# Summing the last 24 upward tiles of a PEER layer from two halves of 512-column matmuls

## What is computed

```python
def blk(args):
    xb, ib, gb = args
    a = jnp.einsum('tkd,td->tk', u_tab[ib], xb, preferred_element_type=f32)
    a = jax.nn.gelu(a, approximate=False) * gb
    return jnp.einsum('tk,tkd->td', a.astype(xb.dtype), v_tab[ib])
```

## Time and profile before

| | |
|---|---|
| median of 3 runs | 1940.96 us (1940.9 to 1941.74) |
| the profiled execution | 1938.03 us |
| its span, from the first to the last instruction | 1936.0 us, mean granted clock 0.994 |
| TensorE busy (matmul) | 1899.6 us, 98% of the span |
| VectorE busy | 1459.9 us, 75% |
| ScalarE busy | 1123.1 us, 58% |
| DMA | 480.75 MB, mean 248 GB/s |

### The profile page before, as it was taken

One profiled execution on the slowest core, in us unless ns is written; L12 is line 12 of the kernel. 1 busy time (PEld: TensorE's weight loads), 2 busy tenths in 40 slices (PEclk: granted clock), 3 DMA queues, 4 the chain that ended last, 5 costly groups with the idle time before them and its releaser, 6 DMA issues.

```text
span 1936.0 us, 41169 instructions
## 1 busy us (share of the span) xinstructions
PE 1899.6 (98%) x11552; PEld 1678.1 (87%) x11552; DVE 1459.9 (75%) x3771; ACT 1123.1 (58%) x2217; POOL 456.1 (24%) x321
## 2 busy tenths in 40 slices
PE   7998999999999999999999999999999999999998
PEld 6848988899999888888888798889999998888887
DVE  5666699987774788888875658899777467777776
ACT  2035468876555555555555555887655555555554
POOL 1000000777776000000000000056777720000000
PEclk9999999999999999999999999999999999999998
DMA  9956388997779999999983235789877988888884
GB/s 381 375 217 251 110 283 283 276 240 196 175 174 222 334 365 360 363 358 360 316 295 89 110 131 180 226 232 237 203 176 174 215 270 268 262 266 268 261 267 166
DMA packets 251005, 480.75 MB, mean 248 GB/s; under 512 B 57120, under 2 KB 156704, under 8 KB 246960
## 3 DMA queue, kind: packets, MB, share of 16 engines
q1 hardware_dynamic: 205536, 426.21, 66.3%
q0 software_dynamic: 45392, 53.60, 12.2%
HBM read 426.10 MB, written 53.61 MB: 248 GB/s over the span
## 4 chain that ended last, share of the span: by engine, by line
PE 95%; ACT 2%; DVE 1%; issue 1%; DMA 0%; SPq 0%; ACTq 0%; DVEq 0%
PE bank L595 94%; ACT big L1115 1%; PE bank L731 0%; DMA raw<-in_x 0%; DVE raw L1337 0%; DVE big L1345 0%; ACT big L1133 0%; DVE wmod_ring L1345 0%; ACT hi L1064 0%; DVE big L1439 0%; ACT L1208 0%; DVE raw L1345 0%; ACT raw L1053 0%; ACT L1184 0%; ACT hi L1184 0%
## 5 line engine op out<-in xcount | busy, mean ns | idle before, releaser
L1639 DVE TENSOR_TENSOR lo<-raw,hi 128x512 fp32r<-128x512 f32 x1024 | 705.6, 689 | 307.1 <-ACT hi L1184 294.3
L595 PE MATMUL bank<-x_both,hi 128*128 128x256 f32 (+1 forms) x3984 | 880.8, 310 | 5.1 <-issue 2.2
L1184 ACT ACTIVATE hi<-raw 128x512 fp32r<-128x512 f32 x1024 | 645.1, 631 | 384.2 <-PE bank L595 375.2
L595 PEld LDWEIGHTS bank<-x_both,hi 128*128 128x128 f32 x3984 | 648.0, 191 | 47.4 <-issue 2.8
L595 PE MATMUL bank<-x_both,lo 128*128 128x256 f32 x2440 | 685.7, 281 | 0.0
L534 POOL DMA_INDIRECT g_store<-far_gate,far_at x256 | 423.5, 1654 | 394.7 <-DVE far_at L1631 246.2
L595 PEld LDWEIGHTS bank<-x_both,lo 128*128 128x128 f32 x2440 | 463.8, 190 | 0.0
L595 PE MATMUL bank<-hi,a_hi 128*128 128x512 f32 x1024 | 398.4, 389 | 0.0
L595 PE MATMUL bank<-lo,a_hi 128*128 128x512 f32 x1024 | 398.4, 389 | 0.0
L595 PE MATMUL bank<-hi,a_lo 128*128 128x512 f32 x1024 | 398.4, 389 | 0.0
L595 PEld LDWEIGHTS bank<-hi,a_hi 128*128 128x128 f32 x1024 | 192.2, 188 | 40.0
(11 more groups left out here) (170 smaller groups left out, 1404.2 us busy)
## 6 DMA issues: line engine op xcount, KB each, us to landing
raw<-in_u SPq DMA_DIRECT2D x256, 512.0 KB
raw<-in_v SPq DMA_DIRECT2D x256, 512.0 KB
s_store<-work SPq DMA_DIRECT2D x256, 128.0 KB
wmod_ring<-s_store SPq DMA_DIRECT2D x256, 128.0 KB, 3.6
wmod_ring<-in_w_mod SPq DMA_DIRECT2D x54, 512.0 KB, 5.1
big<-in_w_mod SPq DMA_DIRECT2D x40, 512.0 KB, 6.4
big<-in_w_q POOLq DMA_DIRECT2D x16, 1024.0 KB, 5.5
g_store<-zero SPq DMA_DIRECT2D x2, 8192.0 KB, 30.7
```

Of the source, the lines that this page charges most:

```text
L595: return nc.tensor.matmul(o, w, x, start=start, stop=stop, skip_group_check=free)
L1184: f(hi[:, r % 2, c], raw[:, r, c], ACT.Copy).then_inc(s[l]["hi_done"], 1)
L1639: v.tensor_tensor(lo[:, r % 2, c], raw[:, r, c], hi[:, r % 2, c].bitcast(F32), ALU.subtract).then_inc(s[l]["lo_done"], 1)
```

## The change

The 24 tiles of the tail take the wide form. `WIDE_ALL` is now the number of wide tiles in a layer, 56 + 24 = 80, and semaphores that count wide tiles go by it; `skipped` takes out the 48 narrow tiles between. The core of the diff:

```diff
+TAIL_AT = GROUP_AT + GROUPS
+WIDE_ALL = WIDE_TILES + NKEY - TAIL_AT
...
                     for r in range(4):
                         up(GROUP_AT + 4 * i + r, r % 2)
                         group(4 * i + r, r)
-                with pe.Fori((GROUP_AT + GROUPS) // 2, NKEY // 2) as i:
-                    for r in range(2):
-                        up(2 * i + r, r)
                 pe.wait_ge(s[l]["g_copied"], GROUPS)
+                for r in range(4):
+                    wide(TAIL_AT + r, r, False)
+                with pe.Fori(TAIL_AT // 4 + 1, NKEY // 4) as i:
+                    for r in range(4):
+                        wide(4 * i + r, r, True, TAIL_AT - WIDE_TILES)
+                pe.wait_ge(s[l]["s_sum"], WIDE_ALL * (l + 1))
                 down(0, 0, first=True)
...
-                up_steps(GROUP_AT + GROUPS, NKEY - 4)
                 for r in range(4):
-                    up_step(NKEY - 4 + r, r, NKEY // 4 - 1)
+                    wide_step(TAIL_AT + r, r, TAIL_AT // 4, True, r >= 1, TAIL_AT - WIDE_TILES)
+                with act.Fori(TAIL_AT // 4 + 1, NKEY // 4 - 1) as i:
+                    for r in range(4):
+                        wide_step(4 * i + r, r, i, True, True, TAIL_AT - WIDE_TILES)
+                for r in range(4):
+                    wide_step(NKEY - 4 + r, r, NKEY // 4 - 1, True, True, TAIL_AT - WIDE_TILES)
+                    if r == 3:
+                        sum_gelu(NKEY - 1, 3, TAIL_AT - WIDE_TILES)
                     if r >= 2:
                         split_a(r - 2, r, r - 2, False)
...
+                for r in range(4):
+                    for half in range(2):
+                        lower(TAIL_AT + r, r, half)
+                    if r >= 2:
+                        sum_halves(TAIL_AT + r - 2, r - 2, TAIL_AT - WIDE_TILES)
+                with dve.Fori(TAIL_AT // 4 + 1, NKEY // 4) as i:
                     for r in range(4):
                         for half in range(2):
                             lower(4 * i + r, r, half)
+                        sum_halves(4 * i + r - 2, (r + 2) % 4, TAIL_AT - WIDE_TILES)
                 dve.wait_ge(s[l]["g_copied"], GROUPS)
                 gates_in(0, 0)
                 for n in range(2):
                     weigh(n, n, 0)
+                    sum_halves(NKEY - 2 + n, n + 2, TAIL_AT - WIDE_TILES)
```

More of the change, by code:

```diff
@@ L867, in experts, with wide @@
             def experts(l):
-                def wide(n, r, wait=True):
+                def wide(n, r, wait=True, skipped=0):
                     if wait:
-                        pe.wait_ge(s[l]["s_sum"], n - 3 + WIDE_TILES * l)
+                        pe.wait_ge(s[l]["s_sum"], n - skipped - 3 + WIDE_ALL * l)
                     o = bank[r][:, :]
@@ L937, in experts @@
                     up(GROUP_AT - 2 + r, r)
-                pe.wait_ge(s[l]["s_sum"], WIDE_TILES * (l + 1))
+                pe.wait_ge(s[l]["s_sum"], WIDE_TILES + WIDE_ALL * l)
                 for r in range(4):
@@ L1190, in half_sum, with sum_gelu, wide_step @@
                     f(work[:, r, :], bank[r][:, T:2 * T], ACT.Copy).then_inc(s[l]["s_half"], 1)
-                def sum_gelu(n, r):
-                    act.wait_ge(s[l]["s_sum"], n + 1 + WIDE_TILES * l)
+                def sum_gelu(n, r, skipped=0):
+                    act.wait_ge(s[l]["s_sum"], n - skipped + 1 + WIDE_ALL * l)
                     f(work[:, r, :], work[:, r, :], ACT.Gelu).then_inc(s[l]["s_gelu"], 1)
-                def wide_step(n, r, round_, wait=True, before=True):
+                def wide_step(n, r, round_, wait=True, before=True, skipped=0):
                     nr, nround = (r + 2) % 4, round_ + (r + 2) // 4
@@ L1201, in wide_step @@
                     if before:
-                        sum_gelu(n - 1, (r + 3) % 4)
+                        sum_gelu(n - 1, (r + 3) % 4, skipped)
                 def gelu(n, r, round_, wait=True):
@@ L1712, in experts, with sum_halves @@
                             lower(tile, tile, half)
-                def sum_halves(n):
-                    dve.wait_ge(s[l]["s_half"], n + 1 + WIDE_TILES * l)
-                    v.tensor_tensor(work[:, n % 4, :], bank[n % 4][:, 0:T], work[:, n % 4, :], ALU.add).then_inc(s[l]["s_sum"], 1)
+                def sum_halves(n, r, skipped=0):
+                    dve.wait_ge(s[l]["s_half"], n - skipped + 1 + WIDE_ALL * l)
+                    v.tensor_tensor(work[:, r, :], bank[r][:, 0:T], work[:, r, :], ALU.add).then_inc(s[l]["s_sum"], 1)
                 for n in range(GROUP_AT - 2):
                     if 1 <= n <= WIDE_TILES:
-                        sum_halves(n - 1)
+                        sum_halves(n - 1, (n - 1) % 4)
                     for half in range(2):
@@ L1739, in experts @@
                         one_hot(4 * i + r, r)
-                with dve.Fori((GROUP_AT + GROUPS) // 4, NKEY // 4) as i:
+                for r in range(4):
[4 more added lines that the diff above has]
+                with dve.Fori(TAIL_AT // 4 + 1, NKEY // 4) as i:
                     for r in range(4):
```

## The result

The changed kernel took **1951.85 us** in the median of 6 runs (1948.66 to 1953.75), the kernel before 1940.93 us (1939.05 to 1942.45) beside it: a ratio of 1.0055, with a 95% interval of 1.0042 to 1.0068. That is 8 to 13 us slower. The forecast was slower by 7.3 us, with 1951.0 as the upper end of the range; the direction was right, the time lies 0.85 us above the range. The profiled run took 1951.48 us, with a span of 1949.7; of before 1938.03 and 1936.0.

A forecast was written before the change was run, and what follows sets the result against it. TensorE was taken to bound the kernel, unbroken from the gate groups through the downward pass. Pace -5.1, start +2.0 and ends +7.9 gave +4.8, with the clock +7.3: 1948.2 us against the median of 1940.96, range 1943.0 to 1951.0.

The forecast's parts named there:

- Start: Start of the tail: TensorE must wait for ScalarE's copy of the last gate group; +1.0 us a layer.
- Pace: Tail tiles: wide 2.774 us against narrow 2.880, 0.106 less a tile, 2.55 us a layer saved; -5.1 in the sum.
- End chain: End of the tail: copy, addition, two lowerings and a_lo precede the first downward matmul; 2.53 us, +1.18 us a layer.
- Late load: End of the tail: tile 129's load delays tile 127's copy; the ends then cost 4.34 (layer 0) and 3.59 us (layer 1).
- Clock: Start of the downward pass: after idles of 4.3 and 3.6 us TensorE's clock falls to half speed; +2.4 us.
- Not late: Rival, end of tail: tile 129's load lands in time, 1.18 us a layer remain, clock holds; 1943.3, chance 0.16.
- Both waits are covered: Rival: the waits at the tail's start and end are hidden and the pace alone is left; 1935.9, faster, chance 0.05.

The follow-up runs named there:

- both4: Changed kernel with the first 4 and last 4 of the 24 tail tiles kept narrow, 16 wide; 1941.01 us, ratio 1.0000 to the kernel before.
- both4l: both4 with layer 0's two modulation loads issued behind the spill of tile 123; 1941.84 us, ratio 1.0010 to the kernel before.
- stall: Changed kernel with one added TensorE wait in mid-tail, ahead of tile 116, for the Gelu of tile 114; one run, 1956.68 us.
- order: Changed kernel with VectorE's two additions of halves (tiles 126, 127) put behind downward tile 0's lowerings and a_lo; 1945.11 us, ratio 1.0024 to before.
- vfirst: Changed kernel with layer 0's two modulation loads issued behind the loads of downward tiles 0 and 1; 1950.02 us, ratio 1.0049 to before.
- late: Changed kernel with layer 0's two modulation loads issued behind downward loads 0 and 1 and the spill of tile 123; 1949.13 us, ratio 1.0043 to before.
- again: The changed kernel run once more, unedited, for a second trace; 1949.73 us.
- warm: Changed kernel with six unused matmuls between the last upward matmul and TensorE's wait for the last addition of halves; 1947.91 us, ratio 1.0035 to before.
- orderl: Changed kernel with the edits of order and late together; 1943.43 us, ratio 1.0017 to the kernel before.
- end4: Changed kernel with the last 4 of the 24 tail tiles kept narrow, 20 wide; 1941.95 us, ratio 1.0007 to the kernel before.
- before2: The kernel before run once more, unedited, for a second trace; 1938.47 us.

## Why the prediction came out as it did

- **Start: right.** 1.02 us a layer by the rows, 1.0 foretold; in both4 and both4l, where narrow tiles cover the copy, the wait is gone.
- **Pace: the step that failed.** 2.55 us a layer was to be saved, 1.27 was. The price 0.106 came from one stretch of layer 1, and I took it for that of the form; so the term -5.1 of the sum was twice too large. The trace of before already held the other price. Its copies in layer 0, five tiles from the first row to the second:

```profile
267.49 0.39 ACT L1190 ACTIVATE work<-bank 128x256 f32<-128x256 f32 x1 [0.42 <-PE bank L595]
...
281.62 0.39 ACT L1190 ACTIVATE work<-bank 128x256 f32<-128x256 f32 x1 [0.20 <-PE bank L595]
```

  That is 2.826 us a tile. The tail ran at this pace in both layers of every kernel whose tail is wide, up to the wait that stall adds. With it the forecast would have been 2.5 us higher and the time inside the range. Why the tail always begins at the slower pace is open. The rule of the Trainium skill that the prediction weighed (page "TensorE: Matmul & The Clock Gate", section "Back-to-back issue gap") gave 0.5 us a layer; the section gives it for a single matmul by itself and has other figures for a stream with weight loads. In the trace a narrow matmul takes 0.120 us (2.880 over 24), the rule says 0.109, and the measured 1.27 lies between the rule and the forecast: the columns are not all that counts.
- **End chain: right.** 2.57 us from copy to matmul against 2.53, and order shows that VectorE's list is its cause.
- **Late load: the mechanism was right in layer 0, its size in part by luck; wrong in layer 1.** In layer 0 the end was foretold as 4.34 and cost 3.81 and 4.78 us in two traces. In the first of them two errors nearly cancel: the split of downward tile 1 came at 646.97 and not at 645.8, and TensorE, at the slower pace, was ready at 646.26 and not at 644.54. vfirst and late show the cause to be SP's queue, though a spill stood ready to take the load's place. In layer 1 I foretold 3.6 us and it is 2.78, an idle of 2.62, in the four traces with this end and no other wait (changed, again, vfirst, late). I left the load at its time of before, while layer 1 itself begins 8 us later (first copy at 1187.66, before 1179.72) and the scatter ended only 2.5 us later (last issue 1563.70, before 1561.20), so the loads had room: SP, which waited 3.7 us for the scatter before, did not wait for it in the first trace and waited 0.9 us in the second. Together the ends were 1.3 us cheaper than foretold.
- **Clock: it fell in both layers, but not as costed.** I let it fall some 3 us into the idle and charged 2.4 us; by that it would have held behind layer 1's 2.62 us. The trace of before already had a fall behind a shorter wait, in layer 1's attention, which the prediction leaves out (TensorE, then the window behind it, clock 0.50):

```profile
1078.64 1.00 PE L731 MATMUL bank<-cst,big 128*128 128x128 f32 x6 [2.14 <-ACT big L1133]
```

```profile
1079.30:1082.30 3.00, 3.00 (x17) 1.91 (x14) 1.45 (x6) 1.60 (x4) 0.00 (x0) 0.50 1.01 429
```

  Behind the tail it was low from the restart on, 3.4 us in each layer, 3.4 us lost. Warm, which removes it alone, came 3.9 us under the changed kernel in the median and 3.1 us by the trace.
- **Net:** the forecast of +7.3 lacks 2.5 for the pace and 1.0 for the clock, and has 1.3 too much for the ends: +9.5. What lies between that and the measured median is within the interval. That the time came within 1 us of the range is luck in part: what the ends had too much hid 1.3 of the 3.5 us that the other two lacked.
- **The rivals.** "Not late" was true of one layer only and did not come to no change, since the clock fell behind 2.62 us. "Both waits are covered" named the right cure: with the lowerings ahead of the additions and the transfers in time, orderl keeps 3.3 of the 10.7 us. That the pace alone then brings 1935.9 is refuted: both4l, with no wait left and 32 wide tiles in the tails, saved 1.63 us by its trace, where 0.106 a tile would make 3.4.

## What to carry to other kernels

Read the price of a form in several stretches of a trace before it is multiplied by a count: here one row gave twice the gain of another, and the gain was the whole reason for the edit. When a step is added behind an engine's last result, look at what stands behind it in the next engine's list, for all of it moves onto the path (1.7 of 2.57 us here, and taken off again by reordering two calls). Where a short wait must stay, try to fill it: here six useless matmuls a layer kept the clock and gave back 3 to 4 us.

## What was not expected of the hardware

- At a granted clock of 1.00 a pair of wide matmuls is 0.347 or 0.353 us apart, one or the other for tens of microseconds. A wait can change it (stall: 2.827 to 2.773 us a tile in both layers), but none is needed: in vfirst it changed near 289 and 343 us, in layer 0's wide stage, where no pair is more than 0.366 us apart. What picks the spacing is open. Narrow tail tiles had 2.88 in both layers of both traces of the kernel before.
- The clock fell behind idle times of 1.79 (order) and 1.80 us (both4), and held behind 1.68 (stall), 1.28 (end4), 1.14 (warm) and 0.93 (order). So an idle far shorter than the 3.39 us of the earlier trace rows can cost 1.7 us more than itself. Its length does not settle it: the wait of 2.13 or 2.14 us in layer 1's attention is in all fourteen traces, and the clock fell behind it in eight, as shown above, and held in six. In before2:

```profile
1079.25 0.89 PE L731 MATMUL bank<-cst,big 128*128 128x128 f32 x6 [2.14 <-ACT big L1133]
```

```profile
1079.30:1082.30 3.00, 3.00 (x26) 2.01 (x28) 2.06 (x8) 2.41 (x6) 0.00 (x0) 1.00 1.00 418
```

- The slow stretch in the norm between the layers, the normalization ahead of layer 1, varies for the same kernel. The mean clock over the same 20 us (1003 to 1023) was 0.74 in the first trace of the changed kernel and 0.83 in the second. With the changing pace of the wide stage this is part of why runs of one kernel lie several microseconds apart.
